# Query norm moved into the scale of the scores, and the scores' masking and maximum done in two passes per head

## What is computed

```python
def odd_mixer(h, w_in, q_norm_w, k_norm_w, sinks, w_out, pos):
    q, k, v, gate = jnp.split(h @ w_in, ...)            # 32 query heads, 4 key heads, 64 wide
    q = rope(rms_norm_2(q, q_norm_w), pos)
    k = rope(rms_norm_2(k, k_norm_w), pos)
    o = swa_sinks(q, k, v, sinks)                       # window of 128 tokens
    return (o * jax.nn.silu(gate)) @ w_out

# swa_sinks, per head, two blocks of 128 tokens
    scores = jnp.einsum('bnihgd,bnjhd->bnhgij', qb, kk) * (d ** -0.5)
    scores = jnp.where(valid, scores, -1e30)
    m = jnp.maximum(jnp.max(scores, axis=-1, keepdims=True), sink)
    p = jnp.exp(scores - m)
    p = p / (jnp.sum(p, axis=-1, keepdims=True) + jnp.exp(sink - m))
```

## Time and profile before

| | us |
|---|---|
| median of three runs | 1888.33 (1888.32 to 1889.33) |
| the profiled execution | 1888.36 |
| its span, first to last instruction | 1886.5 |
| PE busy in it | 1877.8 |
| DVE busy | 1250.4 |
| ACT busy | 998.8 |

### The profile page before, as it was taken

The page is one execution under the profiler, slowest core; times in us unless marked ns, Lnnn a source line. Parts: engine busy times, 40 slices in busy tenths (PEclk is TensorE's granted clock), DMA queues, the critical chain, the costliest instruction groups (busy, mean ns, idle before and its releaser), DMA issues.

```text
span 1886.5 us, 22391 instructions
## 1 busy us (share of the span) xinstructions
PE 1877.8 (100%) x8563; PEld 1547.4 (82%) x8563; DVE 1250.4 (66%) x1781; ACT 998.8 (53%) x1378; POOL 14.4 (1%) x32
## 2 busy tenths in 40 slices
PE   9999999999999999999999999999999999999999
PEld 7888888888888888888888888888888888877777
DVE  6676566776666566665466776755776676787775
ACT  6777554554444344443444455654555555566663
POOL 0001000000000000000000000000000000000000
PEclk9999999999999999999999999999999999999999
DMA  9667764786666666666666686666666587655565
GB/s 323 205 192 179 206 181 154 220 250 193 197 190 195 194 190 191 198 192 195 194 192 195 217 269 195 195 191 181 197 203 195 193 250 225 182 171 168 153 188 173
DMA packets 212362, 375.90 MB, mean 199 GB/s; under 512 B 14672, under 2 KB 35968, under 8 KB 212256
## 3 DMA queue, kind: packets, MB, share of 16 engines
q1 hardware_dynamic: 211008, 371.71, 65.1%
q0 software_dynamic: 816, 2.11, 0.8%
q10 hardware_dynamic: 432, 0.66, 0.1%
HBM read 361.82 MB, written 12.60 MB: 198 GB/s over the span
## 4 chain that ended last, share of the span: by engine, by line
PE 98%; ACT 1%; DMA 0%; issue 0%; DVE 0%; SPq 0%; DVEq 0%; ACTq 0%
PE g L1200 31%; PE g L1201 31%; PE g L1202 31%; PE m L1134 1%; PE ob L1278 0%; PE m L1260 0%; DMA raw<-in_w_in 0%; PE m L1360 0%; PE m L1258 0%; ACT wh L1390 0%; PE ob L1281 0%; PE m L1246 0%; PE ob L1346 0%; PE m L1290 0%; ACT L1528 0%
## 5 line engine op out<-in xcount | busy, mean ns | idle before, releaser
L1667 DVE TENSOR_TENSOR wl<-raw,wh 128x1024 fp32r<-128x1024 f32 (+1 forms) x660 | 802.5, 1217 | 558.7 <-ACT wh L1390 556.0
L1390 ACT ACTIVATE wh<-raw 128x1024 fp32r<-128x1024 f32 (+1 forms) x661 | 695.3, 1053 | 727.7 <-PE g L1202 720.6
L1200 PE MATMUL g<-wh,xh 128*128 128x512 f32 x1886 | 741.1, 393 | 0.1
L1202 PE MATMUL g<-wh,xl 128*128 128x512 f32 x1886 | 734.5, 389 | 0.0
L1201 PE MATMUL g<-wl,xh 128*128 128x512 f32 x1886 | 734.1, 389 | 0.0
L1200 PEld LDWEIGHTS g<-wh,xh 128*128 128x128 f32 x1886 | 354.1, 188 | 78.2 <-issue 4.0
L1202 PEld LDWEIGHTS g<-wh,xl 128*128 128x128 f32 x1886 | 354.0, 188 | 74.4
L1201 PEld LDWEIGHTS g<-wl,xh 128*128 128x128 f32 x1886 | 354.2, 188 | 71.7
L1200 PE MATMUL g<-wh,mh 128*128 128x512 f32 x732 | 288.0, 393 | 0.7 <-DVE wl L1667 0.7
L1202 PE MATMUL g<-wh,ml 128*128 128x512 f32 x732 | 285.2, 390 | 0.0
L1201 PE MATMUL g<-wl,mh 128*128 128x512 f32 x732 | 284.9, 389 | 0.0
(11 more groups left out here) (178 smaller groups left out, 757.4 us busy)
## 6 DMA issues: line engine op xcount, KB each, us to landing
raw<-in_ev_w_in SPq DMA_DIRECT2D x128, 512.0 KB, 3.8
raw<-in_w_in SPq DMA_DIRECT2D x92, 512.0 KB, 4.3
raw<-in_w_gate SPq DMA_DIRECT2D x88, 512.0 KB, 4.4
raw<-in_w_up SPq DMA_DIRECT2D x88, 512.0 KB, 4.4
raw<-in_w_down SPq DMA_DIRECT2D x88, 512.0 KB, 4.7
raw<-in_od_w_in SPq DMA_DIRECT2D x72, 512.0 KB, 4.0
raw<-in_w_out SPq DMA_DIRECT2D x32, 512.0 KB, 4.4
raw<-in_ev_w_out SPq DMA_DIRECT2D x32, 512.0 KB, 4.8
```

What stands on the lines that cost most here:

```text
L1200: e.matmul(o, hi[:, kt, c], h, start=first, stop=False)
L1202: last = e.matmul(o, lo[:, kt, c], h, start=False, stop=end)
L1390: return e.activation(o, i, AF.Copy, scale=scale)
L1667: return e.tensor_tensor(o, a, b, op)
```

## The change

Queries are rotated without having been normalised: `on_norm` is gone for them, `on_sq` is laid right behind `oq_evac`, and the squares go to another buffer; rotation and turns follow, and sum and root are laid beside the turns. The root now gives minus 1/8 of the reciprocal of the root mean square, per token and head (`rsq`). When the scores leave PSUM, one DVE operation per key block (128 and 256 columns, so two for each head) adds the mask, multiplies by that number and takes the minimum along the row with minus the sink as its start (`tensor_tensor_reduce`: out = (in0 + in1) x scale, a second output the minimum of it). The stored scores are negated, and the exponent takes them with scale -1. `omax` keeps only its last small step, and its cost in `WORK` goes from 2.25 to 0.2. `od_quad` now lays the scores once, in one test, the last query turn and the last three turns in `ring` are booked as done and DVE is booked no more than 1.0 us ahead; after eight slots it lays them in any case. Keys go as before.

```diff
...
-        "oqk": (0, 2.2, 1.75), "omax": (0, 2.25, 0), "oexp": (1.28, 0, 0), "oapt": (.62, 0, .45), "oapv": (.6, 0, 1.6),
+        "oqk": (0, 2.2, 1.75), "omax": (0, .2, 0), "oexp": (1.28, 0, 0), "oapt": (.62, 0, .45), "oapv": (.6, 0, 1.6),
...
-            yield from self.od_norm(a[0])
+            say("on_sq", a[0])
...
+                yield from self.room("dve", 2.0)
+                say("on_rope", a[0], k)
+            for k, p in enumerate(("on_sum", "on_root")):
+                yield 2 if k else 1
+                yield from self.made("on_rope", a[0], k)
...
+                yield from self.room("dve", 1.0)
+                say(p, a[0])
...
-        yield from self.free(3)
-        yield from self.room("dve", 1.0)
+        for _ in range(8):
+            if (all(self.end[p] <= self.now for p in [("oq_turn", g // 2, 1)] + self.ring[-3:]) and
+                    self.through["dve"] - self.now <= 1.0):
+                break
+            yield 1
...
+
+        def od_scale(g):
+
+            return rsq[g // 2].rearrange("p (t h) -> p h t", t=2)[:, 4 * (g % 2):4 * (g % 2) + 4, :]
...
-                                            accum_out=sm[:, h, kb:kb + 1])
+                                            scale=-1.0, accum_out=sm[:, h, kb:kb + 1])
...
-                        on.wait_ge(s_orope, nth("on_rope", a[0] - 1 if a[0] else "k", 1))
+                        on.wait_ge(*full("ok_turn", 1))
+                        on.wait_ge(s_on_sum, nth(*p) - 1)
...
-                    act(w3(W1)[:, :, 0:width], T3[:, :, 0:width], AF.Square).then_inc(s_on_sq, 1)
+                    act(w3(squares[a[0]])[:, :, 0:width], T3[:, :, 0:width], AF.Square).then_inc(s_on_sq, 1)
...
-            def root(dst, src, n, width, from_, dst_free=()):
+            def lowest(o, scores, mask, g, i, kb):
+
+                h = 4 * g + i
+                return e.tensor_tensor_reduce(o, scores, mask, od_scale(g)[:, i, kb:kb + 1], nsink[:, h:h + 1],
+                                              ALU.add, ALU.min, mx[:, h, kb:kb + 1])
+
+            def root(dst, src, n, width, from_, dst_free=(), eps=1e-6, sign=1.0):
...
-                on.wait_ge(*steps.mark(e.tensor_scalar(v, src, 1.0 / width, 1e-6, ALU.mult, ALU.add)))
+                on.wait_ge(*steps.mark(e.tensor_scalar(v, src, 1.0 / width, eps, ALU.mult, ALU.add)))
...
-                    on.wait_ge(*steps.mark(stt(q, v, -0.5, y, ALU.mult, ALU.mult)))
+                    turned_about = sign if i == 2 else 1.0
+                    on.wait_ge(*steps.mark(stt(q, v, -0.5 * turned_about, y, ALU.mult, ALU.mult)))
...
-                stt(dst, q, 1.5, y, ALU.add, ALU.mult).then_inc(s_root, 1)
+                stt(dst, q, 1.5 * sign, y, ALU.add, ALU.mult).then_inc(s_root, 1)
...
+                    on.wait_ge(s_root, roots[("on_root", g // 2)])
...
-                        stt(od_probs(g)[:, i, :], od_bank(g, i)[:, 0:384], 64 ** -0.5, C("band"), ALU.mult,
-                            ALU.add).then_inc(s_bank_dve if i < 3 else s_ob_dve, 1)
+                        for kb, (lo, hi) in enumerate(((0, 128), (128, 384))):
+                            last = lowest(od_probs(g)[:, i, lo:hi], od_bank(g, i)[:, lo:hi], C("band")[:, lo:hi], g, i, kb)
+                        last.then_inc(s_bank_dve if i < 3 else s_ob_dve, 1)
...
-                    reduce(mx[:, hs, 0:1], od_probs(g)[:, :, 0:128], ALU.max, True)
-                    on.wait_ge(*steps.mark(reduce(mx[:, hs, 1:2], od_probs(g)[:, :, 128:384], ALU.max, True)))
-                    on.wait_ge(*steps.mark(tt(mx[:, hs, :], mx[:, hs, :],
-                                              nsink[:, hs].unsqueeze(2).to_broadcast([128, 4, 2]), ALU.min)))
...
-                    on.wait_ge(s_on_norm, nth(*p))
+                    if a[0] == "k":
+                        on.wait_ge(s_on_norm, k + 1)
+                    else:
+                        on.wait_ge(*taken(find("oq_evac", a[0])[-1]))
...
+                    on.wait_ge(s_on_sq, nth("on_sq", a[0]))
...
-                    if a[0] != "k":
-                        on.wait_ge(*norm_n)
-                    r0 = rs[:, 0:2 * n]
+                    r0 = rs[:, 0:8] if a[0] == "k" else rsq[a[0]]
...
-                           w3(W1)[:, :, 0:width].rearrange("p t (g d) -> p t g d", d=64),
+                           w3(squares[a[0]])[:, :, 0:width].rearrange("p t (g d) -> p t g d", d=64),
...
-                    n = 8 if a[0] == "k" else 16
-                    root(rs[:, 0:n], rs[:, 0:n], n, 64, (s_on_sum, nth(*p)))
+                    if a[0] == "k":
+                        root(rs[:, 0:8], rs[:, 0:8], 8, 64, (s_on_sum, nth(*p)))
+                    else:
+                        on.wait_ge(s_root, roots[p] - 1)
+                        root(rsq[a[0]], rsq[a[0]], 16, 1, (s_on_sum, nth(*p)), eps=64e-6, sign=-1.0)
...
-                    n = 4 if a[0] == "k" else 8
-                    on.wait_ge(s_root, roots[("on_root",) + a])
+                    on.wait_ge(s_root, roots[("on_root", "k")])
...
-                        v = T3[:, k, 0:64 * n].rearrange("p (g d) -> p g d", d=64)
-                        norm_n = (s_on_norm, 2 * nth(*p) - 1 + k)
-                        tt(v, v, rs[:, n * k:n * k + n].unsqueeze(2).to_broadcast([128, n, 64]),
+                        v = T3[:, k, 0:256].rearrange("p (g d) -> p g d", d=64)
+                        tt(v, v, rs[:, 4 * k:4 * k + 4].unsqueeze(2).to_broadcast([128, 4, 64]),
```

More of the change, by code:

```diff
@@ L875, in program @@
         rsa = st[:, 344:346]
+        rsq = [st[:, 428 + 16 * j:444 + 16 * j] for j in range(4)]
         nsum = st[:, 346:348]
@@ L928, in program @@
         so = A2[:, 0:2048].rearrange("p (r t n) -> p r t n", r=2, t=2)
+        squares = {x: W1 if x == "k" else A1[:, 3584:4608] for x in ("k", 0, 1, 2, 3)}
         tab = {"k": A2[:, 2048:2304].rearrange("p (a k e n) -> p a k e n", a=2, k=2, e=2),
```

## The result

The changed kernel is slower: 1895.77 us (median of 5, 1894.53 to 1897.11) against 1888.33, a ratio of 1.0035 with a 95% interval of 1.0024 to 1.0045 (estimated from all the runs; the two medians alone give 1.0039). The prediction was 1887.5, no change that can be measured; it was wrong in size and sign.

What follows compares the result with a forecast made beforehand. The prediction took PE, busy 1877.8 of 1886.5 us, as the bound, with only its waits able to move. Three waits gone (-3.28) and one meeting in OB (+2.5) gave -0.8, other terms 0: 1887.5 us, range 1884.4 to 1890.6.

Steps and rivals of the forecast that it cites:

- PE is the bound; all that can move is its waits: Whole kernel: PE is busy 1877.8 of 1886.5 us, so removing its waits can gain about 4.0 us at most.
- The 0.2%: Timing: a difference under 0.2% (3.8 us) is about what a measurement can't tell from none.
- The three waits go, -3.28: PE at the scores: the new test leaves no turn open ahead of them, saving 0.95 + 0.75 + 1.58 us.
- one such end, at quad 2: Planner: the eight slots run out behind a turn at g = 2, costing 0.75 to 1.58 us; not counted.
- DVE's work, -9 us, worth nothing: DVE: 33.7 us go out and 24.3 come in, -9 us (-16 to +1); counted 0 for the time.
- The burst: DVE at the scores: a quad's reading grows from 1.87 to 3.0 us (2.2 to 4.3); counted 0, bound +0.6 a quad.
- The order of query work, worth 0, at most +1 us a block: Query steps on DVE and ACT: the new order delays `wl` by two us at most, under 3.16 to spare.
- move forward by 8 to 20 us: Query blocks: the path to the last turn loses some six slots, so quads come 8 to 20 us earlier.
- OB shared by a product and scores, one meeting, +2.5: Buffer OB: `oapv` right behind scores, g = 4 on 2, makes PE wait 2.5 us (1.7 to 3.8), once.
- Several meetings: Rival: products behind scores at several quads, 2.5 us each; 1890.0 for two, 1892.5 for three; 1889 to 1893, chance 0.17.
- The case that the change doesn't do what it says: Rival: DVE stays over 1.0 for eight slots, scores go behind turns as often as now; 1888.3, chance 0.09.
- The sum: Whole kernel: -3.28 + 2.5 = -0.8 us, giving 1887.5 us; chance of the forecast 0.42.

Runs made afterwards that it cites:

- turns_behind_scores: Kernel before, with four turns moved from directly ahead of the scores of quads 1, 4 and 5 to behind them; 1886.38 us, ratio 0.9986.
- passes_only: Kernel before, with only the fused mask-scale-maximum passes in place of the reading and the two reductions; 1889.55 us, ratio 1.0003.
- root_behind_product: Changed kernel, with the query root of block 2 laid behind quad 1's gate product instead of ahead of it; 1890.95 us, ratio 1.0011 to before.
- high_part_later: Changed kernel, with the high parts of quads 0 and 1 moved behind turn copies in ACT's own order only; 1890.09 us, ratio 1.0004 to before.
- scores_by_hand: Changed kernel, with the scores of quads 2 and 5 laid earlier and block 2's second rotation later; 1894.25 us, ratio 1.0030 to before.
- after_again: The changed kernel unchanged, timed and profiled again (the second measurement and second profile); 1894.82 us against 1889.57, ratio 1.0027.
- old_test_and_cost: Changed kernel, with the old test for the scores and the old cost of the maxima (2.25); 1895.27 us, ratio 1.0035 to before.
- old_order_and_test: Changed kernel, with the old order of query work, old test and old cost of the maxima; 1890.00 us, ratio 1.0006 to before.
- banks_by_pair: Changed kernel, with the old order of query work and PE waiting for the scores' banks by pairs of heads; 1886.46 us, ratio 0.9985 to before.
- scores_and_high_part: Changed kernel, with scores of quads 2 and 5 earlier and three high parts behind turn copies in ACT's order; 1886.63 us, ratio 0.9991 to before.

## Why the prediction was wrong, step by step

- **PE is the bound; all that can move is its waits.** Right. Over the kernels above the time follows the waits: -2.9 us at 1.4 or 0.9 of waits, +0.5 at 4.7, +5.3 at 8.1; where it is more than they give, the clock has part in it (last section). The 0.2% that the prediction took as not to be told from none was too wide: the intervals of the table reach some 0.1% to either side.
- **The three waits go, -3.28.** The price was right (`turns_behind_scores`). The step failed in counting what takes their place. The three are gone, yet the eight slots ended behind a turn at quads 2 and 5, 1.79 + 0.89 in the second profile, 1.79 + 0.92 in the first: 2.7 back. The prediction had found one such end, at quad 2, and left it out of its sum, since slips of one slot undo such things: a term put at nothing that measured 2.7. Its price of 0.75 to 1.58 was short at quad 2, since ACT was held at `mh`. With the slots run out, the test never held there: DVE was the condition that failed, not the turns.
- **DVE's work, -9 us, worth nothing.** Right in both halves. A pair of passes starts 0.33 + 0.47 = 0.80 us after the other, against 0.76, as DVE after shows at quad 2:

```profile
1689.47 0.41 DVE L1698 CUSTOM_DVE_ANT_0 PB<-m,small,st 128x128 f32<-128x128 f32 x1 [1.08 <-PE m L1276]
1689.81 0.08 DVE L1698 DVE_READ_ACCUMULATOR2_ANT st<- 128x1 f32 x1
1689.81 0.54 DVE L1698 CUSTOM_DVE_ANT_0 PB<-m,small,st 128x256 f32<-128x256 f32 x1
1690.27 0.08 DVE L1698 DVE_READ_ACCUMULATOR2_ANT st<- 128x1 f32 x1
...
1692.67 1.22 DVE L1684 TENSOR_TENSOR wl<-raw,wh 128x1024 fp32r<-128x1024 f32 x1
```

  The burst is 1692.67 - 1689.47 = 3.2 us against 3.0. The second output is an instruction of its own, 64 of them in the trace. It costs no time of its own here, since the next pass starts with it; what a pass has beyond its columns is 0.33 - 128 x 1.03 ns (the price per column of the reductions) = 0.20 us. The prediction had 0.07 of fixed cost and 0.11 for the output: the sum of the two is nearly right, by luck. The Trainium skill's "VectorE: DVE Perf Modes", section "Two Vector instructions with no wait between them", counts an operation with an accumulator output as two instructions. By that count the burst was to be nearer 3.0 than 2.2 us, and the trace agrees. The Trainium skill's "VectorE: DVE Perf Modes", section "Rules for kernel authors", says that chained operations are not worth fusing for speed. DVE's own time falls by 4.5 us in `passes_only` all the same, the kernel's doesn't.
- **The order of query work, worth 0, at most +1 us a block.** This is the step that failed. It followed a late DVE to one reader, `wl`, with 3.16 us to spare, and weighed ACT's queue only for `on_sq`. DVE has a second reader: ACT's `mh`, which waits for the gated product, and ACT then holds the copies that PE waits for within a half unit. On that path there was some 0.4 us to spare at the largest wait (ACT stood 3.38, PE 2.99). The new order put the root (2.4 us) directly ahead of such a product, which cost 3.0 in one place; `root_behind_product` and `high_part_later` show it from both sides. In the other place, ahead of the scores of quad 2, a rotation and a low part stood ahead of the product, and ACT's stop made 0.9 of the 1.79 (`high_part_later`; `root_behind_product` leaves it as it is). The trace of before had the stops to be seen: there, too, ACT sat idle 9.5 us in five of them at `mh`, none where PE waited. Nor do the quads move forward by 8 to 20 us, save three of the eight: the second scores start at 1652.81 in place of 1669.15, but the first at 1643.60 in place of 1641.09 and the last at 1802.34 in place of 1801.72.
- **OB shared by a product and scores, one meeting, +2.5.** Two meetings, 1.23 + 0.77 = 2.0: the sum is nearly right by luck, with count, price and cause each off. The prediction had the test pass at once and the product of quad g-2 behind the scores of g. In the trace it is the product of quad g-1, and it stands there because the slots had run out: the turn ahead of the scores is that quad's last. Moving the scores alone (`scores_by_hand`) takes both kinds of wait away. Each meeting is cheaper than forecast because a half unit, and at quad 4 a turn as well, lay between.
- **The rivals.** "Several meetings", 1889 to 1893, had the right sign, but its two meetings at what they measured would have left 1888.3 - 3.3 + 2.0 = 1887.0; expired slots and the held `mh` made the loss. The case that the change doesn't do what it says (0.09) named what happened at quads 2 and 5, DVE over 1.0 for eight slots, but its time of 1888.3 has nothing else in it. No rival had ACT's queue in it.
- **The sum.** -3.7 + 2.0 + 2.7 + 3.0 + 0.4 = +4.4 from the waits, where -0.8 was forecast; 1892.7. The waits are thus 4.4 of the measured 5.3 (second measurement) and 7.4 (first); in the second profile most of the rest is the clock (last section), in the first the parts at the start and the end.

What stays open: the first measurement has 2.1 us beyond the second (7.4 against 5.3). Of these 1.2 are the kernel before, which took 1888.33 first and 1889.57 beside the second. The other 0.9 may be the clock, the start or the end; one profile of each doesn't tell how they share it. That the test's room on DVE (1.0) or the number of slots would do better with other values wasn't tried.

## What to carry to other kernels

When a step on one engine is moved, follow every reader of everything behind it on that engine, and then what stands in the reader's own queue: the cost lay two queues away (DVE's root, ACT's high part, PE's product). In an in-order queue an instruction that waits for another engine should stand behind the copies that the bound engine is about to need. A scheduling rule that gives up after some slots puts the work exactly where it meant to keep it from; its price is that of the collision, and the place is best chosen by hand or the wait moved to the part that needs it.

## What the runs showed of the hardware

Not forecast was a cost of PE's waits that comes after them: the clock that it is then granted. Busy time by engine in `after_again` around the wait of 3.0 us; the third number from the right is the granted clock:

```profile
1712.00:1715.50 3.50, 3.50 (x20) 2.87 (x20) 3.05 (x15) 0.12 (x2) 0.00 (x0) 1.00 0.51 165
1715.50:1719.00 3.50, 0.52 (x3) 0.09 (x1) 2.42 (x3) 3.50 (x6) 0.00 (x0) 1.00 0.01 4
1719.00:1722.00 3.00, 2.99 (x17) 2.05 (x18) 1.70 (x4) 1.21 (x5) 0.00 (x0) 0.55 0.76 199
1722.00:1725.00 3.00, 3.00 (x13) 2.38 (x13) 1.81 (x2) 2.04 (x6) 0.00 (x0) 0.88 0.43 151
```

Behind the wait PE is busy for three us at 0.55 and three at 0.88, most of the first at the lower level of 1.2 GHz: by estimate 3 x 0.45 + 3 x 0.12 = 1.7 us of lost work, about the 1.6 that this profile takes longer than the first from the turn at 1612 to the last product (1889.19 - 1611.84 against 1888.33 - 1612.56). The first profile of the same kernel has the same wait and 1.00 in the same stretches:

```profile
1715.50:1719.00 3.50, 1.23 (x6) 0.66 (x4) 2.55 (x4) 2.83 (x4) 0.00 (x0) 1.00 0.19 73
1719.00:1722.00 3.00, 2.28 (x20) 1.68 (x21) 2.20 (x5) 2.25 (x8) 0.00 (x0) 1.00 0.57 168
```

So the fall comes in some executions and not in others. `scores_by_hand` (0.50 in the 2.7 us behind its wait of 3.0) and `old_test_and_cost` (0.65 in the 3.5 us behind its wait of 2.9) show it as well, and of the experiments these two lie furthest above what their waits give: 5.1 us over the kernel before where 2.9 more are waited, 6.0 where it is 4.2. It doesn't take a wait of 3 us. In `old_order_and_test` PE waits 0.3 and then 1.7 us, and is busy for 2.36 of the 4 us before the fall:

```profile
1692.00:1696.00 4.00, 2.36 (x12) 1.47 (x10) 3.97 (x17) 0.60 (x1) 0.00 (x0) 1.00 0.59 217
1696.00:1698.00 2.00, 1.70 (x16) 1.17 (x16) 1.22 (x5) 0.00 (x0) 0.00 (x0) 0.81 0.00 0
1698.00:1700.00 2.00, 2.00 (x8) 1.50 (x5) 0.11 (x1) 1.67 (x3) 0.00 (x0) 0.50 0.00 0
```

In the profiles of `root_behind_product` and `high_part_later`, whose longest waits are 1.8 and 1.2 us, the granted clock stays at 1.00 behind them. The mean granted clock of every timed execution, to three places, bears this out. It is under 1.000 in 7 of 13 executions of the changed kernel, where those of `after_again` take 1894.9 to 1896.2 us against 1893.2 to 1894.7 at 1.000. It is under 1.000 in 1 of 11 with the root moved, in 1 of 11 with ACT's order moved, and in none of `turns_behind_scores`, `banks_by_pair` and `scores_and_high_part`. In all executions of `scores_by_hand` and `old_test_and_cost` it is under. So taking the wait of 3.0 away did keep the clock in most executions; but with 7 of 11 under in `old_order_and_test` the length of the longest wait doesn't decide by itself, and what does is not shown.
